# Gated linear attention's recurrence on one core: one state update per tile of 128 tokens in place of one per chunk of 64

## The reference

```
cum = cumsum(log_alpha within a chunk)
q_dec  = q * exp(cum)          k_inv = k * exp(-cum)
scores = where(causal, q_dec @ k_inv.T, 0)
o      = scores @ v + q_dec @ state
state  = state * exp(cum_last) + (k * exp(cum_last - cum)).T @ v
```

## Time and profile before

| | |
|---|---|
| median of 3 runs | 2426.56 us (2423.97 to 2426.67) |
| the profiled execution's own time | 2427.1 us |
| its span | 2425.4 us |
| mean granted TensorE clock | 0.987 of full speed |
| TensorE matmul busy | 2338.6 us, 96% of the span |
| VectorE busy | 1085.1 us, 45% |
| ScalarE busy | 886.2 us, 37% |
| GpSimd busy | 263.9 us, 11% |

### The profile page before, as it was taken

The page is one execution under the profiler, slowest core; times in us unless marked ns, Lnnn a source line. Parts: engine busy times, 40 slices in busy tenths (PEclk is TensorE's granted clock), DMA queues, the critical chain, the costliest instruction groups (busy, mean ns, idle before and its releaser), DMA issues. The chain is left out here.

```text
span 2425.4 us, 28794 instructions
## 1 busy us (share of the span) xinstructions
PE 2338.6 (96%) x11732; PEld 1943.9 (80%) x11732; DVE 1085.1 (45%) x1473; ACT 886.2 (37%) x1381; POOL 263.9 (11%) x278
## 2 busy tenths in 40 slices
PE   7999999999999899999999899989999999999998
PEld 7886788878888678888778767877788888888887
DVE  4313388845232368862632243234433344343434
ACT  4221487734322267762533122223222222222232
POOL 0095200000047500000003000000000000000000
PEclk9999999999999999999999999999999999999999
DMA  5111000033211000013411100033111111115231
GB/s 192 41 47 35 1 1 1 1 131 130 80 53 43 10 1 1 1 36 104 141 35 52 47 15 1 34 132 105 52 47 39 52 52 52 40 47 182 89 136 69
DMA packets 104051, 141.36 MB, mean 58 GB/s; under 512 B 11574, under 2 KB 64998, under 8 KB 103942
## 3 DMA queue, kind: packets, MB, share of 16 engines
q1 hardware_dynamic: 103942, 139.84, 17.4%
HBM read 123.05 MB, written 16.78 MB: 58 GB/s over the span
## 5 line engine op out<-in xcount | busy, mean ns | idle before, releaser
L190 PE MATMUL ps<-w_hi,hT_hi 128*128 128x512 f32 (+1 forms) x1760 | 681.4, 387 | 16.0 <-PEq L89 6.0
L192 PE MATMUL ps<-w_hi,hT_lo 128*128 128x512 f32 (+1 forms) x1760 | 675.2, 384 | 0.0
L191 PE MATMUL ps<-w_lo,hT_hi 128*128 128x512 f32 (+1 forms) x1760 | 675.2, 384 | 0.0
L180 DVE TENSOR_TENSOR w_lo<-w_raw,w_hi 128x2048 fp32r<-128x2048 f32 x90 | 207.7, 2308 | 573.4 <-ACT w_hi L164 570.9
L190 PEld LDWEIGHTS ps<-w_hi,hT_hi 128*128 128x128 f32 x1760 | 333.6, 190 | 83.5 <-issue 11.7
L192 PEld LDWEIGHTS ps<-w_hi,hT_lo 128*128 128x128 f32 x1760 | 333.6, 190 | 65.0
L191 PEld LDWEIGHTS ps<-w_lo,hT_hi 128*128 128x128 f32 x1760 | 333.9, 190 | 63.3 <-issue 0.5
L164 ACT ACTIVATE w_hi<-w_raw 128x2048 fp32r<-128x2048 f32 x72 | 137.8, 1913 | 532.2 <-PE ps L192 532.2
L190 PE MATMUL ps<-hT_hi,w_hi 128*128 128x512 f32 x832 | 325.4, 391 | 5.0 <-DVE X L2323 2.7
L192 PE MATMUL ps<-hT_hi,w_lo 128*128 128x512 f32 x832 | 325.1, 391 | 0.0
L191 PE MATMUL ps<-hT_lo,w_hi 128*128 128x512 f32 x832 | 325.0, 391 | 0.0
(11 more groups left out here) (188 smaller groups left out, 2419.6 us busy)
## 6 DMA issues: line engine op xcount, KB each, us to landing
w_raw<-in_w_in SPq DMA_DIRECT2D x22, 1024.0 KB, 5.2
w_raw<-in_ffn_w_up SPq DMA_DIRECT2D x44, 512.0 KB, 4.9
w_raw<-in_ffn_w_down SPq DMA_DIRECT2D x22, 1024.0 KB, 4.9
x_mid<-X SPq DMA_DIRECT2D x24, 512.0 KB, 2.9
w_raw<-in_gla_w_in SPq DMA_DIRECT2D x12, 1024.0 KB, 5.3
X<-in_x SPq DMA_DIRECT2D x16, 512.0 KB, 7.0
w_raw<-in_w_out SPq DMA_DIRECT2D x8, 1024.0 KB, 6.7
X<-x_mid SPq DMA_DIRECT2D x16, 512.0 KB, 7.1
```

What stands on the lines that cost most here:

```text
L180: engine.tensor_tensor(self.p.w_lo[:, slot, 0:size], self.p.w_raw[:, slot, 0:size], plane(self.p.w_hi[:, slot, 0:size]), ALU.subtract).the ...
L190: nc.tensor.matmul(out, a_hi, b_hi, start=first, stop=False)
L191: nc.tensor.matmul(out, a_hi, b_lo, start=False, stop=False)
L192: return nc.tensor.matmul(out, a_lo, b_hi, start=False, stop=last)
```

## The change

The recurrence keeps tiles of 128 tokens, and the state is now updated once a tile. The keys and queries still carry decays counted from the start of their own chunk of 64, so three factors are put in:

- `KM`, made by ScalarE (`key_map`): the first chunk's keys times that chunk's decay, and a plain copy of the second chunk's keys. Queries of the second chunk meet `KM`, queries of the first chunk meet `K`. So `tile_scores` has eight matmuls of 64 moving columns where there were four of 128, and the mask is the plain causal one.
- `KE`, made by GpSimd in one product a tile: `KM` times the second chunk's decay. It is transposed and copied as before, in a step of its own (`turn_keys`).
- the queries of the second chunk are multiplied in place by the first chunk's decay, by GpSimd (`q_scaled`), once the scores have read them.
- `DT`, the decay of a whole tile, is one small GpSimd product.

`keys_values(t)` takes all 128 token rows, `from_state(t)` all 128 queries, each once a tile. The first tile has no product with the state, the first state is a copy out of PSUM, and the last tile has no state update, no transposed keys and no wait for one. The memset of the first state is gone.

```
-            for t in range(TT):
-                if t >= 2:
-                    pool.wait_ge(ke_turned, t - 1)
-                out = KE[:, t % 2, :, :].rearrange("p h (c s) -> p h c s", s=CH)
-                k_in = K[:, :, t * P:(t + 1) * P].rearrange("p h (c s) -> p h c s", s=CH)
-                for c in range(2):
-                    ins = nc.gpsimd.tensor_tensor(out[:, :, c, :], k_in[:, :, c, :],
-                                                  DEC[:, :, 2 * t + c].unsqueeze(2).to_broadcast([P, GH, CH]),
-                                                  ALU.mult)
-                    ins.then_inc(ke_done, 1)
+            nc.gpsimd.tensor_tensor(DT[:], DECv[:, :, :, 0], DECv[:, :, :, 1], ALU.mult).then_inc(dt_done, 1)
+            for t in range(TT):
+                if t + 1 < TT:
+                    pool.wait_ge(km_done, t + 1)
+                    if t >= 1:
+                        pool.wait_ge(ke_turned, t)
+                    nc.gpsimd.tensor_tensor(KE[:], KM[:, t % 2, :, :],
+                                            DEC[:, :, 2 * t + 1].unsqueeze(2).to_broadcast([P, GH, P]), ALU.mult
+                                            ).then_inc(ke_done, 1)
+                if t >= 1:
+                    pool.wait_ge(s_ready, t + 1)
+                    q = Q[:, :, t * P + CH:(t + 1) * P]
+                    nc.gpsimd.tensor_tensor(q, q, DEC[:, :, 2 * t].unsqueeze(2).to_broadcast([P, GH, CH]), ALU.mult
+                                            ).then_inc(q_scaled, 1)
...
+                    nc.tensor.matmul(prog.ps[:, 0, h * P:h * P + CH], K[:, h, t * P:(t + 1) * P],
+                                     Q[:, h, t * P:t * P + CH], start=(h == 0), stop=True, skip_group_check=True)
+                pe.wait_ge(km_done, t + 1)
+                for h in range(GH):
+                    mm = nc.tensor.matmul(prog.ps[:, 0, h * P + CH:(h + 1) * P], KM[:, t % 2, h, :],
+                                          Q[:, h, t * P + CH:(t + 1) * P], start=False, stop=True,
...
+            def turn_keys(t):
+                pe.wait_ge(ke_done, t + 1)
+                if t >= 1:
+                    pe.wait_ge(ke_taken, t)
...
+            def keys_values(t):
+                pe.wait_ge(ke_taken, t + 1)
+                if t >= 1:
+                    pe.wait_ge(st_done, GH * t)
...
+            def from_state(t):
+                pe.wait_ge(st_done, GH * t)
+                pe.wait_ge(q_scaled, t)
...
-            pe.wait_ge(st_zero, 1)
             tile_scores(0)
+            turn_keys(0)
             for t in range(TT):
-                pe.wait_ge(ke_taken, t + 1)
-                keys_values(t, 0)
+                if t + 1 < TT:
+                    keys_values(t)
+                    tile_scores(t + 1)
+                if t + 2 < TT:
+                    turn_keys(t + 1)
                 within(t)
-                from_state(t, 0)
-                if t + 1 < TT:
-                    tile_scores(t + 1)
-                keys_values(t, 1)
-                from_state(t, 1)
-
-            pe.wait_ge(st_done, GH * NCH)
+                if t:
+                    from_state(t)
+
+            pe.wait_ge(s_done, TT)
+            pe.wait_ge(ke_taken, TT - 1)
+            pe.wait_ge(st_done, GH * (TT - 1))
...
+            def key_map(t):
+                if t >= 2:
+                    act.wait_ge(s_ready, t - 1)
+                    act.wait_ge(ke_done, t - 1)
+                for h in range(GH):
+                    nc.scalar.activation(KM[:, t % 2, h, 0:CH], K[:, h, t * P:t * P + CH], ACT.Copy,
+                                         scale=DEC[:, h, 2 * t:2 * t + 1])
+                nc.scalar.activation(KM[:, t % 2, :, CH:P], K[:, :, t * P + CH:(t + 1) * P], ACT.Copy
+                                     ).then_inc(km_done, 1)
+
+            key_map(0)
+            key_map(1)
             for t in range(TT):
-                act.wait_ge(ke_turned, t + 1)
-                if t >= 2:
-                    act.wait_ge(kv_ready, 2 * t - 2)
-                nc.scalar.activation(KEt[:, t % 2, :, :], prog.ps[:, 1, :].rearrange("p (h d) -> p h d", h=GH),
-                                     ACT.Copy).then_inc(ke_taken, 1)
+                if t + 1 < TT:
+                    act.wait_ge(ke_turned, t + 1)
+                    if t >= 2:
+                        act.wait_ge(kv_ready, t - 1)
+                    nc.scalar.activation(KEt[:, t % 2, :, :], prog.ps[:, 1, :].rearrange("p (h d) -> p h d", h=GH),
+                                         ACT.Copy).then_inc(ke_taken, 1)
+                if t + 2 < TT:
+                    key_map(t + 2)
                 if t >= 1:
                     head_squares(t - 1)
             head_squares(TT - 1)
...
+            def state(t):
+                dve.wait_ge(kv_ready, t + 1)
+                if t == 0:
+                    nc.vector.tensor_copy(ST[:, 1, :, :].rearrange("p (a b) v -> p a (b v)", a=2), prog.ps[:, 2:4, :]
+                                          ).then_inc(st_done, GH)
+                    return
...
             mask_scores(0)
             for t in range(TT):
-                state(t, 0)
                 if t + 1 < TT:
+                    state(t)
                     mask_scores(t + 1)
-                state(t, 1)
                 if t >= 1:
                     normed(t - 1)
```

More of the change, by code:

```diff
@@ L1728, in gla_core @@
     kb = prog.B
-    NCH = SEQ // CH
     f = kb + 32
     S = prog.at("S", [P, 2, GH, P], f)
-    KE = prog.at("KE", [P, 2, GH, P], f + 4)
+    KM = prog.at("KM", [P, 2, GH, P], f + 4)
     KEt = prog.at("KEt", [P, 2, GH, P], f + 8)
+    KE = prog.at("KE", [P, GH, P], f + 12.5)
+    DT = prog.at("DT", [P, GH, TT], prog.S + 0.5625)
+    DECv = DEC[:].rearrange("p h (t c) -> p h t c", c=2)
     stat = prog.at("stat", [P, 3, TT, GH], f + 12)
@@ L1753, in gla_core @@
     masked = prog.sem("masked")
-    st_zero = prog.sem("st_zero")
+    dt_done = prog.sem("dt_done")
+    q_scaled = prog.sem("q_scaled")
     s_ready = prog.sem("s_ready")
     s_done = prog.sem("s_done")
+    km_done = prog.sem("km_done")
     ke_done = prog.sem("ke_done")
@@ L1788, in _ @@
                                     fill=0.0, base=0, pattern=[[1, P]], channel_multiplier=-1).then_inc(masked, 1)
-            pool.wait_ge(masked, 1)
-            nc.gpsimd.memset(mask[0:CH, CH:P].bitcast(F32), 0.0).then_inc(masked, 1)
+            nc.gpsimd.tensor_tensor(DT[:], DECv[:, :, :, 0], DECv[:, :, :, 1], ALU.mult).then_inc(dt_done, 1)
             for t in range(TT):
-                if t >= 2:
-                    pool.wait_ge(ke_turned, t - 1)
-                out = KE[:, t % 2, :, :].rearrange("p h (c s) -> p h c s", s=CH)
-                k_in = K[:, :, t * P:(t + 1) * P].rearrange("p h (c s) -> p h c s", s=CH)
-                for c in range(2):
-                    ins = nc.gpsimd.tensor_tensor(out[:, :, c, :], k_in[:, :, c, :],
-                                                  DEC[:, :, 2 * t + c].unsqueeze(2).to_broadcast([P, GH, CH]),
-                                                  ALU.mult)
-                    ins.then_inc(ke_done, 1)
+                if t + 1 < TT:
[10 more added lines that the diff above has]
+                                            ).then_inc(q_scaled, 1)
         @block.tensor
@@ L1807, in tile_scores @@
                 for h in range(GH):
-                    mm = nc.tensor.matmul(prog.ps[:, 0, h * P:(h + 1) * P], K[:, h, t * P:(t + 1) * P],
-                                          Q[:, h, t * P:(t + 1) * P], start=(h == 0), stop=True,
+                    nc.tensor.matmul(prog.ps[:, 0, h * P:h * P + CH], K[:, h, t * P:(t + 1) * P],
[4 more added lines that the diff above has]
+                                          Q[:, h, t * P + CH:(t + 1) * P], start=False, stop=True,
                                           skip_group_check=True)
                 mm.then_inc(s_ready, 1)
-                pe.wait_ge(ke_done, 2 * t + 2)
+            def turn_keys(t):
+                pe.wait_ge(ke_done, t + 1)
                 if t >= 1:
@@ L1815, in tile_scores @@
                 for h in range(GH):
-                    mm = nc.tensor.transpose(prog.ps[:, 1, h * P:(h + 1) * P], KE[:, t % 2, h, :], prog.ident[:])
+                    mm = nc.tensor.transpose(prog.ps[:, 1, h * P:(h + 1) * P], KE[:, h, :], prog.ident[:])
                 mm.then_inc(ke_turned, 1)
[L1819 to L1823, removed]
+            def keys_values(t):
+                pe.wait_ge(ke_taken, t + 1)
+                if t >= 1:
+                    pe.wait_ge(st_done, GH * t)
                 for h in range(GH):
-                    mm = nc.tensor.matmul(prog.ps[:, 2 + h // 2, h % 2 * DV:(h % 2 + 1) * DV], KEt[rows, t % 2, h, :],
-                                          V[rows, t, h * DV:(h + 1) * DV], start=(h % 2 == 0), stop=True,
+                    mm = nc.tensor.matmul(prog.ps[:, 2 + h // 2, h % 2 * DV:(h % 2 + 1) * DV], KEt[:, t % 2, h, :],
```

(47 more changed lines are left out.)

## The result

The median fell from 2426.86 us (six runs, 2423.97 to 2428.37) to 2386.06 us (six runs, 2384.47 to 2390.26). The ratio is 0.9834, 95% interval 0.9822 to 0.9847: 40.8 us or 1.7% faster. Forecast were 2393.4 us and a range of 2386 to 2403; the direction and the mechanism held, the gain was some 7 us larger than the sum. So the time lies only 0.06 us inside the range, and outside the 2390 to 2397 that the prediction gave its own case.

What follows compares the result with a forecast made beforehand. TensorE's own work was taken to bound the kernel (11.1 us a tile plus a 0.68 wait). With 8.18 us tiles, the stage gains 32.3 and the clock 0.9: 2427.1 to 2393.9, less 0.5 to the median, 2393.4 us; range 2386 to 2403.

Steps and rivals of the forecast that it cites:

- its own case: Whole kernel: TensorE's own work in sequence gives 2393.4 us, own range 2390 to 2397, chance 0.70.
- rival 2: Scores: short matmuls cost by their moving columns, so half the price, 7 us less, 2386.4 us; chance 0.06.
- rival 3: Scores: weight loads not hidden behind short matmuls, 1.26 us more a tile, 2402.2 us; chance 0.08.
- Rival 4: Recurrence loop: a new wait each tile on ScalarE, late `KEt`, 5 to 7 us, 2399 us; chance 0.10.
- Rival 5: Recurrence: TensorE's clock falls to 0.50 though busy, 2445.7 us if throughout; chance 0.04.
- That costs nothing by the rows ... I take 1.92 for both remaining groups: Each tile's keys times values and product with the state: twice the rows or loaded columns, still 1.92 us each.
- tiles 1 to 5: Recurrence on TensorE: five tiles of 8.18 us each, 40.9 us together.
- tile 6: Recurrence on TensorE: no transposes behind it, 7.54 us.
- tile 7: Recurrence on TensorE: only `within` and the product with the state, 3.85 us.
- The clock's term: Start of the recurrence: an earlier turn to full clock gains 0 to 3.3 us more; 0.9 taken.

Runs made afterwards that it cites:

- a2: Changed kernel with eight more ScalarE activations of 64 elements in each key map from tile 2 on, output unused: tile 7.36 us, stage 60.13, whole 2390.56 us.
- s1: Changed kernel with a tile's scores in four matmuls of 128 moving columns, not eight of 64, all against K: tile 6.51 us, median 2380.37 us.
- b1_ends: Kernel before, without the product with the zero state and the last chunk's keys times values and update: 2423.12 against 2424.83 us, ratio 0.9995; stage 94.95.
- w1: Changed kernel with 22 unused 512-column matmuls ahead of the barrier before the stage, where TensorE idles 5.4 us: stage 61.39, median 2385.64 us.
- w2: Changed kernel with the 22 matmuls before the barrier and 13 more in tile 0's waits: stage 57.99, median 2384.83 us.

## Why the prediction was right, and where its sum was short

**Right.** TensorE's own work set the tile before, but for 0.68 us, and sets it after; no wait recurs in the loop. The wait for `KEt` went, the additions on ScalarE, VectorE and GpSimd are hidden (a2), and a short fp32 matmul costs the same step with 64 as with 128 moving columns (s1). Per tile, 4.42 us went: the wait 0.68, two groups 2 x 1.73, six changes of shape 1.12, less 0.84 for the scores. Rivals 2 and 3 fell: the score step is 0.11, the same for 64 and 128 moving columns. Rival 4 fell, nothing waits for `KEt` in the loop. Rival 5 fell too, the clock was 1.00 from 1398.3 to the end of the stage.

**Luck.** That the total lies where rival 2 put it (2386.4), and the tile at 7.36 where it was to be 7.3 by rival 2 and 8.2 by the forecast, is a coincidence: by the tile alone one would have called it rival 2, and only the score step and s1 say otherwise. The lower end of the range was there for rival 2; the forecast's own mechanism was given 2390 to 2397, and the time is 4 us below that.

**Short.** The step that failed is "That costs nothing by the rows ... I take 1.92 for both remaining groups". I read 1.92 and 1.93 for a group on 64 rows and one on all rows as proof that the shape is free. Both held the price of a change of shape, since each stood beside a group of another shape. The remaining three groups cost 1.73 each, the transposes 0.44 to 0.45 where I took 0.64, the scores 1.73 for 1.78: 7.36 and not 8.18. The account of the missing us: tiles 1 to 5, 5 x 0.82 = 4.1; tile 6, 7.54 - 6.97 = 0.6; tile 7, 3.85 - 3.26 = 0.6. From the stage's start to keys times values of tile 1 I had 15.4 and it took 13.05; of these 2.4 I had credited 0.9 to the clock, so 1.5 more. Of the 1.5, the turn at 9.5 in place of 13.1 us is 0.9 (1.8 less the 0.9 credited), keys times values of tile 0 starting 5.2 instead of 5.6 us into the stage is 0.3 (the key map took 1.46 for 1.7), and `within` of tile 0 is 0.2. Together 6.8; 33.2 + 6.8 = 40.0, as measured. The clock's term was mis-sized for the reason named in the prediction, the 64-row groups, which I gave too little weight. One figure of rival 5 is wrong and enters no sum: scores and transposes are 2.42 of the forecast tile's 8.18, that is 30% and not 24.

## What to carry to other kernels

Look at the shape column of neighbouring matmul groups: where rows or loaded columns alternate between 64 and 128, each change cost 0.17 to 0.19 us of TensorE here (fp32, clock at 1.00), and a group's distance to the next includes it, so price a group from a place where its neighbours have the same shape. Going from 128 to 64 moving columns saved nothing while 128 columns were loaded, so a split into halves doubled the price of the scores; here it was worth paying (0.84 us a tile for two groups of 1.73). And read a stage's own length beside the total: here 2 to 5 us in a stage did not show clearly in the median, and the clock behind the stage accounts for it in b1_ends.

## What the runs showed of the hardware that was not expected

A single 64-row matmul between full ones costs 0.39 us more than the same one on all rows (two changes), a 64-column one 0.34. Matmuls on 64 of 128 rows early in a stage put off the return to 2.4 GHz: 17.4 us after the start against 9.6, with TensorE busy in both. The low stretches around the stage's start had only three lengths in twelve kernels, 10.2, 13.7 and 20.5 us. A filled idle time before a stage does not keep the clock by itself: in w1 it fell 3.1 us into the stage (1392.6, the stage began at 1389.51), after waits of TensorE of 1.08, 0.33 and 0.18 us; with such waits in tile 0 filled as well (w2) it stayed at 1.00.
